# An SSD stage with its sample states turned, C unscaled, and the carried state faded on GpSimd

## The chip, the cores and the metric

The kernel runs on one core of a Trainium2 chip. The metric is the device time of one execution in microseconds (us).

## The reference, cut to what matters

One layer of a decoder trunk is computed for a prompt of 1024 tokens and for 8 samples of one token each: a half-step FFN, a mixer, a second half-step FFN. The mixer has a sparse attention branch and an SSD (state space) branch. The change lies in the SSD branch alone, which is, for 32 heads of 64 in 4 groups, with a state of 128 per head and chunks of 128 tokens:

```python
def step(h, inp):                       # one chunk of 128 tokens
    xc, dtc, Bc, Cc = inp
    acs = jnp.cumsum(dtc * Ar, axis=1)
    seg = acs[:, :, None] - acs[:, None, :]
    decay = jnp.exp(jnp.where(tril, seg, -jnp.inf))
    xdt = xc * dtc[..., None]
    cb = jnp.einsum('blgn,bsgn->blsg', Cc, Bc)
    y_diag = jnp.einsum('blsg,blsgr,bsgrp->blgrp', cb, decay, xdt)
    y_off = jnp.einsum('blgn,bgrpn,blgr->blgrp', Cc, h, jnp.exp(acs))
    to_end = jnp.exp(acs[:, -1:] - acs)
    h_new = jnp.exp(acs[:, -1])[..., None, None] * h + jnp.einsum('bsgn,bsgr,bsgrp->bgrpn', Bc, to_end, xdt)
    return h_new, y_diag + y_off
...
y = y + d_skip[:, None] * xs
y = y.reshape(b, T, D_INNER) * silu(z)
y = group_rmsnorm(y) * norm_ssd
```

A sample is one token on a given state: its state is faded by exp(dt A), B times x dt is added, and the sum with C is its output. The new states are outputs of the kernel.

## The kernel before, in words

The program is a row of phases (FFN, projections and scores, time steps, the dense projections, the SSD stage, gathers, attention, FFN). Between two phases all engines meet at a barrier. Inside a phase each engine has its own program, written out by hand, and engines wait for each other by semaphores with counts; an engine works through its program strictly in order, so the order of the lines is the order of the work. `eng.wait_ge(sem, UP + n)` holds an engine's queue until n events have been counted.

`time_steps` (line 1594) computes dt, the running sums `acs` of dt A inside a chunk, `etot` (the exponential of a chunk's whole sum) and `te`, and stores `acs` turned, by head and token, in DRAM for later.

`ssd_groups` (line 2110) goes through 32 steps, n = 0 to 31: group n // 8, chunk n % 8 (`N = SG * TB`). In a step:

- SP loads the chunk's x, B and C (`st`), the sums `acs` spread over all partitions (`ab`) and the gate (`zt`), and loads and stores sample states (`H`).
- TensorE's `turn` (2242) transposes x and B and forms C times B into pB. `through` (2252) multiplies B with the weighted x into pH, what the chunk adds to the carried state, and then forms the output pY: for each head `xdt` times `E` (inside the chunk) and the carried state `hT` times `Cs` (what came before it). `total` (2271) sums squares for the norm.
- ScalarE's `decays` (2337) makes `E`, the exponentials of the differences, in eight shifts and one exponential, and `Cs`, the exponentials of the sums themselves; `decay` fades a sample state unit in four instructions.
- GpSimd's `weigh` makes `xw`; `scale` (2386) multiplies `Cs` by C for eight heads; `read` (2392) multiplies a sample unit with C.
- VectorE's `enter` (2412) makes `xdt` and cuts C times B to the triangle (`cbm`); `states` (2423) adds pH to the faded state `hd` (its sum is `hT`); `weigh` (2443) multiplies E with cbm; `skip` (2448) adds d_skip times x to pY; `fade` (2434) fades the carried state; `gate`, `update` (2456) and `reduce` (2466) follow.

The sample states are cut into 32 units of 128 partitions (two heads' inner index) by 4 samples by 128 state entries, one unit a step, two steps late (`LAG = 2`). At the end of each group VectorE makes a diagonal of the inverse roots, TensorE spreads it over the partitions (`broadcast`), and VectorE normalises the group. VectorE's order is this:

```python
for i in range(N + LAG + 1):
    enter(i + 2); states(i); weigh(i + 1); skip(i); fade(i + 1)
    gate(i); update(i - LAG); reduce(i - LAG - 1)
    ...
```

(written here without the tests on i that cut the ends off, and `...` for the norms.)

Of the kernel before, what the change touches and what calls it, by code (L numbers as in the profile page):

```python
# [1593 lines left out]
def time_steps(nc, d, o, scr, tok, dt, te, etot, acs, upper, ident, constants):  # L1594
# [3 lines left out]
    with Phase(nc, "ts") as ph:  # L1598
# [4 lines left out]
        turn = ph.sb("turn", [P, 2, P])  # L1603
# [13 lines left out]
        @block.sync  # L1617
        def _(sp):
            sp.dma_start(rows[:, 0], d["dt_bias"]).then_inc(r_in, 16)
            sp.dma_start(rows[:, 1], d["a_log"]).then_inc(r_in, 16)  # L1620
            sp.dma_start(upper[:], d["upper"]).then_inc(r_in, 16)
            for dst, src in constants:
                sp.dma_start(dst[:], d[src]).then_inc(others, 16)
            sp.dma_start(o["conv_old"], d["conv_old"]).then_inc(others, 16)
            sp.wait_ge(moved, UP + 1)
            sp.dma_start(scr["acs"].rearrange("(j q) l -> q j l", j=2), turn[:]).then_inc(stored, 16)
            sp.wait_ge(moved, UP + 2)
            sp.dma_start(scr["steps"].rearrange("v h b -> h v b"), steps[:]).then_inc(stored, 16)
            sp.wait_ge(stored, UP + 32)
            sp.wait_ge(others, UP + 16 * (len(constants) + 1))  # L1630

        @block.scalar
        def _(act):
# [11 lines left out]
            act.wait_ge(exped, UP + 5)  # L1645
# [464 lines left out]
def ssd_groups(nc, d, o, scr, h, S, dt, te, etot, acs, upper, dskip, nssd, smc, zsm, ones, ident):  # L2110
# [4 lines left out]
    N, UNITS = SG * TB, SG * GT * 2  # L2115
    RS, RZ, RH, HB = 4, 3, 4, NB // 2
    LAG = 2
    with Phase(nc, "sg") as ph:
        st = ph.sb("st", [P, RS, XT, P])
        zt = ph.sb("zt", [P, RZ, GT, P])  # L2120
        ab, E, Cs = (ph.sb(n, [P, 2, R, P]) for n in ("ab", "E", "Cs"))
        xdt, xw = (ph.sb(n, [P, 3, GW]) for n in ("xdt", "xw"))
        bt, cbm = ph.sb("bt", [P, 3, 2 * P]), ph.sb("cbm", [P, 2, P])
        hT, hd = (ph.sb(n, [P, 2, GW]) for n in ("hT", "hd"))
        sq = ph.sb("sq", [P, 2, GT, P])
        root, diag = ph.sb("root", [P, N + SG]), ph.sb("diag", [P, TB, P])
        eps = ph.sb("eps", [P, 1])
        H, T = ph.sb("H", [P, RH, HB, DS]), ph.sb("T", [P, 2, HB, DS])
        bc = ph.sb("bc", [P, 2, 2, HB, DS])
        bcs = ph.sb("bcs", [NB, 2, SG, DS])  # L2130
        steps = ph.sb("steps", [P, 2, SG * GT, NB])
        xd, sk, ys, sqs = (ph.sb(n, [P, SG, GT, NB]) for n in ("xd", "sk", "ys", "sqs"))
        diag8 = ph.sb("diag8", [NB, SG, NB])
        pX, pB, pH, pR = (ph.ps(n, [P, 512]) for n in ("pX", "pB", "pH", "pR"))
        pY, pD = ph.ps("pY", [P, 2, 512]), ph.ps("pD", [P, 2, 512])
        st_in = [ph.sem(f"st_in{q}") for q in range(RS)]
        z_in = [ph.sem(f"z_in{q}") for q in range(RZ)]
        ab_in, bc_in = ([ph.sem(f"{n}{q}") for q in range(2)] for n in ("ab_in", "bc_in"))
        H_in, H_out = ([ph.sem(f"{n}{q}") for q in range(RH)] for n in ("H_in", "H_out"))
        yd = [ph.sem(f"yd{x}") for x in range(2)]  # L2140
        turned, x_dt, cb_m, copied, grown, exped, weighed, x_w, c_s, h_d, h_mm, hup, skipped, gated, squared, summed = (
            ph.sem(n) for n in ("turned", "x_dt", "cb_m", "copied", "grown", "exped", "weighed", "x_w", "c_s", "h_d", "h_mm", "hup",
                                "skipped", "gated", "squared", "summed"))
        rooted, inv, diagd, spread, scaled, decayed, updated, multd, reduced, small, rows_t, rows_m, rows_s, ssm_saved, ch_s, tail, fallen = (
            ph.sem(n) for n in ("rooted", "inv", "diagd", "spread", "scaled", "decayed", "updated", "multd", "reduced", "small", "rows_t",
                                "rows_m", "rows_s", "ssm_saved", "ch", "tail", "fallen"))
        block = ph.block()
        flat = lambda a: a.rearrange("p r l -> p (r l)")
        v3 = lambda a: a.rearrange("p (r e) -> p r e", r=R)
        wide = lambda a, n: a[:, n % TB, n // TB * R:(n // TB + 1) * R].unsqueeze(2).to_broadcast([P, R, PD])  # L2150
# [13 lines left out]
        def _(sp):  # L2164
            def chunk(n):
                if n >= RS:
                    sp.wait_ge(skipped, UP + n - RS + 1)
                    sp.wait_ge(c_s, UP + later(n - RS))
                sp.dma_start(st[:, n % RS], scr["xc"][n // TB, n % TB]).then_inc(st_in[n % RS], 16)
# [6 lines left out]
            def sums(n):  # L2176
                if n >= 2:
                    sp.wait_ge(exped, UP + n - 1)
                    sp.wait_ge(grown, UP + later(n - 2))
# [3 lines left out]
            def state(m, io):  # L2183
                g, half, t = unit(m)
                return io[g].rearrange("p (t b e) -> p t b e", t=GT, b=NB)[:, t, half * HB:(half + 1) * HB]

            def load_state(m):
                if m >= RH:
                    sp.wait_ge(H_out[m % RH], UP + 16 * (m // RH))
                    sp.wait_ge(multd, UP + m - RH + 1)  # L2190
                sp.dma_start(H[:, m % RH], state(m, d["state_ssm"])).then_inc(H_in[m % RH], 16)

            def load_rows(k):
                if k >= 2:
# [8 lines left out]
            for v in range(2):  # L2203
                for x in range(2):
                    src = bass.AP(scr["steps"].tensor, (v * SH + x) * NB, [[0, PD], [2 * NB, SG * GT], [1, NB]])
                    sp.dma_start(steps[x * PD:(x + 1) * PD, v], src).then_inc(small, 16)
            for n in range(2, RS):
                chunk(n)
            for n in range(RZ):
# [3 lines left out]
            sp.wait_ge(rows_m, UP + 1)  # L2213
            sp.dma_start(scr["bcs"].rearrange("v g b e -> b v g e"), bcs[:]).then_inc(rows_s, 16)
            sp.wait_ge(rows_s, UP + 16)
            load_rows(0)
            load_rows(1)
            for i in range(N + LAG + 2):
                if 2 <= i + 2 < N:
                    sums(i + 2)  # L2220
                if RS <= i + RS - 1 < N:
                    chunk(i + RS - 1)
                if RZ <= i + RZ - 1 < N:
                    gate(i + RZ - 1)
                m = i - 1 - LAG
                if 0 <= m < UNITS:
                    sp.wait_ge(updated, UP + m + 1)
                    sp.dma_start(state(m, o["ssm_s"]), H[:, m % RH]).then_inc(H_out[m % RH], 16)
                    if m >= 1 and m - 1 + RH < UNITS:
                        load_state(m - 1 + RH)  # L2230
                    if m % GT == GT - 1 and m // GT + 2 < UNITS // GT:
                        load_rows(m // GT + 2)
# [3 lines left out]
            for q in range(RH):  # L2236
                sp.wait_ge(H_out[q], UP + 16 * (UNITS // RH))
# [3 lines left out]
        def _(pe):  # L2241
# [10 lines left out]
            def through(n):  # L2252
                pe.wait_ge(copied, UP + n + 1)
                pe.wait_ge(x_w, UP + n + 1)
                pe.wait_ge(hup, UP + n)
                nc.tensor.matmul(pH[:], bt[:, n % 3, 0:P], xw[:, n % 3], start=True, stop=True).then_inc(h_mm, 1)
                pe.wait_ge(weighed, UP + n + 1)
                pe.wait_ge(c_s, UP + later(n))
                pe.wait_ge(skipped, UP + n - 1) if n >= 2 else pe.wait_ge(rows_m, UP + 1)
                first = n % TB == 0  # L2260
                for t in range(GT):
                    for k in range(1 if first else 2):
                        for x in range(2):
                            r = 2 * t + x
                            lhs, rhs = (xdt[:, n % 3], E[:, n % 2, r]) if k == 0 else (hT[:, (n - 1) % 2], Cs[:, n % 2, r])
                            m = nc.tensor.matmul(pY[PD * x:PD * (x + 1), n % 2, t * P:(t + 1) * P], lhs[:, r * PD:(r + 1) * PD], rhs,
                                                 start=k == 0, stop=first or k == 1)
                            if t == GT - 1 and (first or k == 1):
                                m.then_inc(yd[x], 1)

            def total(n):
                pe.wait_ge(squared, UP + n + 1)
                if n % TB == 0:
                    pe.wait_ge(rooted, UP + n // TB)
# [4 lines left out]
            def broadcast(g):  # L2279
                pe.wait_ge(diagd, UP + TB * (g + 1))  # L2280
                pe.wait_ge(scaled, UP + GT * g)
                for c in range(TB):
                    m = nc.tensor.matmul(pD[:, c // 4, c % 4 * P:(c % 4 + 1) * P], ones[:], diag[:, c], start=True, stop=True)
                m.then_inc(spread, 1)

            for v in range(2):
                for g in range(SG):
                    m = nc.tensor.transpose(pY[0:NB, v, g * P:(g + 1) * P], smc[:, g * XT + GT + v], ident[:])
            m.then_inc(rows_t, 1)
            turn(0)  # L2290
            turn(1)
            for i in range(N + 2):
# [4 lines left out]
                if i >= 2:  # L2297
                    total(i - 2)
                if i >= TB + 5 and (i - 5) % TB == 0 and i <= N:
                    broadcast((i - 5) // TB - 1)  # L2300
# [6 lines left out]
            broadcast(SG - 1)  # L2307
# [5 lines left out]
        def _(act):  # L2313
            def copy(n):
                act.wait_ge(turned, UP + n + 1)
                if n >= 3:
                    act.wait_ge(h_mm, UP + n - 2)
                    act.wait_ge(cb_m, UP + n - 2)
# [7 lines left out]

            def decay(m):
                g, half, t = unit(m)
                act.wait_ge(H_in[m % RH], UP + 16 * (m // RH + 1))
                if m == 0:  # L2330
                    act.wait_ge(small, UP + 64)
                for b in range(HB):
                    at = half * HB + b
# [786 lines left out]
```

## Time and profile before

| | us |
|---|---|
| three runs | 4072.28, 4075.02, 4075.45 (median 4075.02) |
| the profiled execution: its own time | 4073.7 |
| its span, first to last instruction | 4071.9 |
| TensorE busy | 3724.5 (91%) |
| VectorE busy | 1986.9 (49%) |
| ScalarE busy | 943.4 (23%) |
| GpSimd busy | 358.0 (9%) |

The profile page gives one execution. Shares are of the whole span, which has stages with different limits; the SSD stage begins at 2017.9 us, VectorE's last instruction in it starts at 2324.0.
### The profile page before, as it was taken

To read this page: it belongs to the slowest core of one execution; us is meant where nothing else is said; L and a number is where in the kernel's file an instruction comes from. 1 tells how busy PE (TensorE), PEld (TensorE's weight loads), DVE (VectorE), ACT (ScalarE), POOL (GpSimd) and SP (SyncE) were. 2 spreads that over 40 slices of the span, in tenths; PEclk is the share of its full clock that TensorE was granted. 3 is DMA by queue.
4 is the path that set the end of the run, shared out by engine and by line. 5 is a ranking of instruction groups with operands and counts; after the bars stand their busy time and mean duration, and the time that the engine had idled before them with its cause. 6 is when DMAs were issued, how large, how long until landed. Compare 5 with 4: busy or idle time off the path is not lost. (4 is left out here: it accounts for less than half of the span.)

```text
span 4071.9 us, 48044 instructions
## 1 busy us (share of the span) xinstructions
PE 3724.5 (91%) x18116; PEld 2942.2 (72%) x18116; DVE 1986.9 (49%) x4404; ACT 943.4 (23%) x2079; POOL 358.0 (9%) x372
## 2 busy tenths in 40 slices
PE   5999999998996999999777589789899999999997
PEld 3888888885654888888655456445467888888886
DVE  3444444442123888764299732244441354453544
ACT  2111111112131222221377400156300221111111
POOL 0000000000000000000055411354100000000000
PEclk8999999998998999999888699899989999999999
DMA  4333343215441132222367332200114022222222
GB/s 182 121 124 124 117 153 124 103 66 192 115 110 68 53 104 84 83 84 83 101 221 221 114 108 81 71 16 11 60 49 152 11 93 83 83 94 77 90 83 83
DMA packets 178142, 406.45 MB, mean 100 GB/s; under 512 B 25896, under 2 KB 104952, under 8 KB 156648
## 3 DMA queue, kind: packets, MB, share of 16 engines
q1 hardware_dynamic: 162264, 360.48, 26.6%
q10 hardware_dynamic: 12448, 21.78, 1.5%
q0 software_dynamic: 3200, 21.11, 1.4%
q8 instruction: 145, 2.38, 0.2%
q14 instruction: 85, 0.70, 0.1%
HBM read 335.35 MB, written 68.14 MB: 99 GB/s over the span
## 5 line engine op out<-in xcount | busy, mean ns | idle before, releaser
L659 ACT ACTIVATE f_u<-f_Y 128x258 f32<-128x258 f32 x408 | 157.2, 385 | 1093.1 <-PE f_Y L558 1093.1
L785 DVE TENSOR_TENSOR f_g<-f_u,f_Z 128x258 f32<-128x258 f32 x136 | 57.6, 424 | 390.7 <-PE f_Z L558 390.7
L1114 PE MATMUL ps_pp<-h,ps_w 128*128 128x344 f32 x720 | 219.0, 461 | 19.9 <-DMA ps_w<-in_w_att 19.9
L1114 PEld LDWEIGHTS ps_pp<-h,ps_w 128*128 128x128 f32 x720 | 136.0, 192 | 100.2 <-DMA ps_w<-in_w_att 20.3
L755 DVE TENSOR_TENSOR f_g<-f_u,f_X 128x258 f32<-128x258 f32 x136 | 57.6, 423 | 299.3 <-PE f_X L558 293.4
L558 PE MATMUL f_Y<-h,raw 128*128 128x258 f32 x704 | 171.2, 387 | 13.6 <-PEq L111 13.6
L558 PE MATMUL f_Y<-f_a,raw 128*128 128x258 f32 x704 | 170.9, 384 | 6.2 <-issue 6.2
L558 PE MATMUL f_Y<-f_tc,f_sums 128*128 128x258 f32 x704 | 167.5, 380 | 1.9 <-issue 1.2
L558 PE MATMUL f_Y<-f_a,f_sums 128*128 128x258 f32 x704 | 168.8, 380 | 0.0
L558 PE MATMUL f_Y<-f_tc,raw 128*128 128x258 f32 x704 | 167.7, 380 | 0.9 <-ACT f_u L659 0.9
L558 PE MATMUL f_X<-h,raw 128*128 128x258 f32 x704 | 168.1, 382 | 0.0
L558 PE MATMUL f_Y<-h,f_sums 128*128 128x258 f32 x704 | 167.5, 381 | 0.5 <-ACT f_u L659 0.5
L558 PE MATMUL f_Z<-h,f_sums 128*128 128x258 f32 x704 | 167.5, 380 | 0.0
L558 PE MATMUL f_Z<-f_tc,f_sums 128*128 128x258 f32 x704 | 167.5, 380 | 0.0
L558 PE MATMUL f_Z<-f_a,f_sums 128*128 128x258 f32 x704 | 162.9, 380 | 0.0
L558 PEld LDWEIGHTS f_Y<-h,raw 128*128 128x128 f32 x704 | 133.2, 192 | 40.7 <-issue 22.1
L1917 ACT ACTIVATE S<-dn_Y 128x258 f32<-128x258 f32 x168 | 64.4, 383 | 411.6 <-PE dn_Y L1857 411.6
L558 PEld LDWEIGHTS f_Y<-f_a,raw 128*128 128x128 f32 x704 | 133.2, 190 | 29.5 <-issue 10.3
L558 PEld LDWEIGHTS f_Y<-f_tc,f_sums 128*128 128x128 f32 x704 | 132.8, 189 | 22.7 <-issue 2.7
L558 PEld LDWEIGHTS f_Y<-f_tc,raw 128*128 128x128 f32 x704 | 133.1, 189 | 21.5 <-ACT f_u L659 1.8
L558 PEld LDWEIGHTS f_X<-h,raw 128*128 128x128 f32 x704 | 134.3, 191 | 19.6
L558 PEld LDWEIGHTS f_Y<-h,f_sums 128*128 128x128 f32 x704 | 133.2, 189 | 20.7 <-ACT f_u L659 0.9
(433 smaller groups left out, 7356.5 us busy)
## 6 DMA issues: line engine op xcount, KB each, us to landing
raw<-in_w_f1i SPq DMA_DIRECT2D x44, 1024.0 KB, 4.9
raw<-in_w_f2i SPq DMA_DIRECT2D x44, 1024.0 KB, 4.8
f_wa<-in_w_ada SPq DMA_DIRECT2D x14, 2048.0 KB, 9.7
dn_raw<-in_w_dense SPq DMA_DIRECT2D x28, 1024.0 KB, 5.6
raw<-in_w_f1o SPq DMA_DIRECT2D x16, 1024.0 KB, 4.9
sg_ab<-scr_acs SPq DMA_DIRECT2D x32, 512.0 KB, 5.4
raw<-in_w_f2o SPq DMA_DIRECT2D x16, 1024.0 KB, 4.8
scr_xc<-dn_cv SPq DMA_DIRECT2D x24, 512.0 KB, 4.4
```

The lines of the kernel that those rows point to most:

```text
L558: m = nc.tensor.matmul(bank[i % 2][:, 0:SUB], left[:, k], column(i, which, k), start=fresh and k == 0, stop=k == kp - 1, skip_group_check= ...
L659: nc.scalar.activation(u[:, i % 2, n], bank[i % 2][:, 0:SUB], ACT.Copy).then_inc(done, 1)
L755: nc.vector.tensor_tensor(g[:, i % 2, 0], u[:, i % 2, 0], X[i % 2][:, 0:SUB], ALU.add).then_inc(xread, 1)
L785: nc.vector.tensor_tensor(g[:, i % 2, 1], u[:, i % 2, 1], Z[i % 2][:, 0:SUB], ALU.add).then_inc(zread, 1)
L1114: m = nc.tensor.matmul(pp[n % 2][:, 0:NC], w[:, t % WR, k], h[:, k, c * NC:(c + 1) * NC], start=k == 0, stop=k == KT - 1)
L1917: nc.scalar.activation(u[:, i % 2, n], Y[i % 2][:, 0:SUB], ACT.Copy).then_inc(done, 1)
```

## The change

In `time_steps` the turned sums also go through an exponential on ScalarE, and the result is stored beside them (`eacs`). In `ssd_groups`:

- C is no longer scaled: `Cs`, its exponential on ScalarE and its multiply on GpSimd are gone. The carried state times C goes into a bank of its own, pC, four products for the eight heads; VectorE multiplies pC by the stored exponentials (`carried`, loaded by SP's `growth` as `ea`) and adds pY (`join`).
- The skip moves to TensorE: pY begins with a diagonal of d_skip (`dskips`, made on GpSimd once a group) times x. pY has one buffer instead of two.
- The triangle is cut on GpSimd (`cut`), in bt itself.
- The fading of the carried state goes from VectorE to GpSimd.
- A unit of sample states is now one sample of one group, with the state entries on partitions and the 512 inner entries along them. GpSimd fades it in one multiply (`decay`); TensorE forms B times x dt into pU (`grow`, 8 rows deep, with all but one sample's B masked to zero), VectorE adds pU (`update`), and TensorE forms the output, state times C, as columns of pR (`read`). The arrays in DRAM are laid out to match.
- The norm's broadcast goes in two halves through one bank, and ScalarE copies each to SBUF (`keep`). `zt` has two buffers instead of three.

The core of the diff:

```diff
@@ time_steps
+            sp.wait_ge(exped, UP + 6)
+            sp.dma_start(scr["eacs"].rearrange("(j q) l -> q j l", j=2), grown[:]).then_inc(stored, 16)
...
+            act.wait_ge(moved, UP + 1)
+            nc.scalar.activation(grown[:], turn[:], ACT.Exp).then_inc(exped, 1)
@@ ssd_groups, SP
+            def growth(n):
+                k = later(n) - 1
+                if k >= 2:
+                    sp.wait_ge(mulled, UP + k - 1)
+                for x in range(2):
...
+                    sp.dma_start(ea[x * PD:(x + 1) * PD, k % 2], src).then_inc(ea_in[k % 2], 16)
@@ TensorE
+                if n % TB:
+                    pe.wait_ge(mulled, UP + later(n) - 1)
+                    for t in range(GT):
+                        m = nc.tensor.matmul(pC[:, t * P:(t + 1) * P], hT[:, (n - 1) % 2, t * P:(t + 1) * P], st[:, q, GT + 1], start=True, stop=True)
+                    m.then_inc(c_mm, 1)
+                pe.wait_ge(joined, UP + n)
...
+            def grow(m):
+                pe.wait_ge(updated, UP + m)
+                pe.wait_ge(b_masked, UP + m // NB + 1)
+                nc.tensor.matmul(pU[:], bmask[:, m // NB % 2, m % NB], xrow[:, m // NB], start=True, stop=True).then_inc(u_mm, 1)
+            def read(m):
+                pe.wait_ge(updated, UP + m + 1)
+                for t in range(GT):
...
+            for i in range(N + LAG + 2):
                 if i + 2 < N:
                     turn(i + 2)
                 if i < N:
                     through(i)
...
+                if 0 <= i - LAG - 1 < N:
+                    read(i - LAG - 1)
+                if 0 <= i - LAG + 1 < N:
+                    grow(i - LAG + 1)
+                if 2 <= i < N + 2:
                     total(i - 2)
@@ GpSimd
+            for i in range(N + LAG):
                 if i + 2 < N:
+                    cut(i + 2)
                     weigh(i + 2)
                 if i + 1 < N and (i + 1) % TB:
-                    scale(i + 1)
-                if 0 <= i - LAG < UNITS:
-                    read(i - LAG)
+                    fade(i + 1)
+                if i % TB == 3 and i // TB + 1 < SG:
+                    mask_rows(i // TB + 1)
+                if i % TB == 4 and i // TB + 1 < SG:
+                    skip_rows(i // TB + 1)
+                if 0 <= i - LAG + 1 < N:
+                    decay(i - LAG + 1)
@@ VectorE
             def states(n):
                 dve.wait_ge(h_mm, UP + n + 1)
                 dve.wait_ge(h_d, UP + later(n))
-                wait_y(dve, n)
+                dve.wait_ge(c_mm, UP + later(n))
...
+            def update(m):
+                dve.wait_ge(decayed, UP + m + 1)
+                dve.wait_ge(u_mm, UP + m + 1)
+                nc.vector.tensor_tensor(H[:, m % RH], H[:, m % RH], pU[:], ALU.add).then_inc(updated, 1)
...
                 if i < N:
-                    skip(i)
-                if i + 1 < N and (i + 1) % TB:
-                    fade(i + 1)
+                    if i % TB:
+                        carried(i)
+                    join(i)
                 if i < N:
                     gate(i)
-                if 0 <= i - LAG < UNITS:
+                if 0 <= i - LAG < N:
                     update(i - LAG)
```

How the order of instructions changes on two engines. First TensorE, in the loop of `ssd_groups`, from the end of one step's pY to the next step's: before, pR is the sum of squares (`total`), pX and pB the turn, pH the chunk's state (the numbers of stages are semaphores).

```order
L2276 MATMUL sg_pR<-ones,sg_sq 128x1 [waits stage35]
L2276 MATMUL sg_pR<-ones,sg_sq 128x1 x3
L2248 MATMUL sg_pX<-ident,sg_st 128x128 [waits stage24,stage22,stage3]
L2248 MATMUL sg_pX<-ident,sg_st 128x128 x3
L2249 MATMUL sg_pB<-ident,sg_st 128x128
L2250 MATMUL sg_pB<-sg_st 128x128
L2256 MATMUL sg_pH<-sg_xw,sg_bt 128x512 [waits stage32,stage28,stage24]
```

The same place after the change; pR with smc and H is `read`, pU is `grow`, which waits for stage44 (`updated`) and stage50 (`b_masked`), and pC is the carried state times C.

```order
L2283 MATMUL sg_pR<-smc,sg_H 128x1 [waits stage44]
L2283 MATMUL sg_pR<-smc,sg_H 128x1 x3
L2277 MATMUL sg_pU<-sg_xrow,sg_bmask 128x512 [waits stage50,stage44]
L2290 MATMUL sg_pR<-ones,sg_sq 128x1 [waits stage34]
L2290 MATMUL sg_pR<-ones,sg_sq 128x1 x3
L2244 MATMUL sg_pX<-ident,sg_st 128x128 [waits stage23,stage21,stage3]
L2244 MATMUL sg_pX<-ident,sg_st 128x128 x3
L2245 MATMUL sg_pB<-ident,sg_st 128x128
L2246 MATMUL sg_pB<-sg_st 128x128
L2253 MATMUL sg_pH<-sg_xw,sg_bt 128x512 [waits stage29,stage26,stage23]
L2257 MATMUL sg_pC<-sg_st,sg_hT 128x128 [waits stage31]
```

Between pY and the turn, `read` and `grow` have come in ahead of `total`, each behind a wait for VectorE's updates, and pC stands behind pH.

Then VectorE, one step of its loop, before the change, from xdt (`enter`) to the reduction (ys).

```order
L2417 TENSOR_TENSOR sg_xdt<-sg_pX,dt 128x512 [waits stage20,stage28,stage19,stage21]
L2421 TENSOR_TENSOR sg_cbm<-sg_bt,upper 128x128 [waits stage24,stage27]
L2432 TENSOR_TENSOR sg_hT<-sg_hd,sg_pH 128x512 [waits stage19,stage20,stage30,stage31]
L2446 TENSOR_TENSOR sg_E<-sg_E,sg_cbm 128x1024 [waits stage23,stage26]
L2452 SCALAR_TENSOR_TENSOR h<-sg_st,dskip,sg_pY 128x128 [waits stage20,stage19]
L2452 SCALAR_TENSOR_TENSOR h<-sg_st,dskip,sg_pY 128x128 x3
L2436 TENSOR_TENSOR sg_hd<-sg_hT,etot 128x512 [waits stage32]
L2441 TENSOR_TENSOR h<-h,sg_zt 128x4x128 [waits stage4,stage33]
L2462 SCALAR_TENSOR_TENSOR sg_H<-sg_bc,sg_xd,sg_H 128x128 [waits stage10,stage42]
L2462 SCALAR_TENSOR_TENSOR sg_H<-sg_bc,sg_xd,sg_H 128x128 x3
L2469 TENSOR_REDUCE sg_ys<-sg_T 128x4 [waits stage44]
```

After the change: stage30 is `c_mm`, stage31 `mulled`, stage32 `joined`, stages 18 and 19 the two halves of pY.

```order
L2463 TENSOR_TENSOR sg_xdt<-sg_pX,dt 128x512 [waits stage19,stage26,stage18,stage20]
L2474 TENSOR_TENSOR sg_hT<-sg_hd,sg_pH 128x512 [waits stage30,stage27,stage28]
L2479 TENSOR_TENSOR sg_E<-sg_E,sg_bt 128x1024 [waits stage22,stage24]
L2486 TENSOR_TENSOR h<-sg_pC,sg_ea 128x4x128 [waits stage9,stage30]
L2492 TENSOR_TENSOR h<-h,sg_pY 128x4x128 [waits stage31,stage19,stage18]
L2499 TENSOR_TENSOR h<-h,sg_zt 128x4x128 [waits stage4,stage32]
L2504 TENSOR_TENSOR sg_H<-sg_H,sg_pU 128x512 [waits stage43,stage42]
```

The mask, the skip, the fading and the reduction are gone; the state sum waits for pC's end (stage30), and the one add of pU stands last in the step.

## Rows read from the trace of the kernel before

**Rows 1.** Stretches of the SSD stage: us, busy us (instructions) per engine, PEclk, DMA share, GB/s
```profile
2080.00:2120.00 40.00, 29.81 (x261) 22.73 (x261) 39.97 (x80) 34.09 (x85) 24.95 (x15) 0.87 0.75 245
2120.00:2160.00 40.00, 29.49 (x237) 23.36 (x236) 39.97 (x80) 31.88 (x79) 28.05 (x15) 0.87 0.75 211
2160.00:2200.00 40.00, 30.89 (x227) 24.19 (x224) 39.97 (x76) 33.38 (x81) 22.80 (x14) 0.73 0.75 243
2200.00:2240.00 40.00, 28.80 (x241) 21.94 (x241) 39.93 (x83) 30.20 (x78) 22.53 (x14) 0.88 0.72 220
```

**Rows 2.** Timeline of VectorE, one step: start, us, engine, line, operation, out<-in, shapes
```profile
2129.57 0.68 DVE L2432 TENSOR_TENSOR sg_hT<-sg_hd,sg_pH 128x512 f32<-128x512 f32 x1
...
2136.56 0.68 DVE L2417 TENSOR_TENSOR sg_xdt<-sg_pX,dt 128x512 f32<-128x512 f32 x1
2137.16 0.38 DVE L2421 TENSOR_TENSOR sg_cbm<-sg_bt,upper 128x128 f32<-128x128 f32 x1
2137.46 0.68 DVE L2432 TENSOR_TENSOR sg_hT<-sg_hd,sg_pH 128x512 f32<-128x512 f32 x1
2138.06 1.46 DVE L2446 TENSOR_TENSOR sg_E<-sg_E,sg_cbm 128x1024 f32<-128x1024 f32 x1
2139.44 1.11 DVE L2452 SCALAR_TENSOR_TENSOR h<-sg_st,dskip,sg_pY 128x128 f32<-128x128 f32 x4
2140.48 1.81 DVE L2436 TENSOR_TENSOR sg_hd<-sg_hT,etot 128x512 f32<-128x512 f32 x1
2142.21 0.68 DVE L2441 TENSOR_TENSOR h<-h,sg_zt 128x512 f32<-128x512 f32 x1
2142.81 1.13 DVE L2462 SCALAR_TENSOR_TENSOR sg_H<-sg_bc,sg_xd,sg_H 128x128 f32<-128x128 f32 x4
2143.86 0.67 DVE L2469 TENSOR_REDUCE sg_ys<-sg_T 128x4 f32<-128x512 f32 x1
```

**Rows 3.** Timeline of VectorE: the first and the last state sum of the stage
```profile
2038.24 0.69 DVE L2430 COPY sg_hT<-sg_pH 128x512 f32<-128x512 f32 x1
...
2298.72 0.68 DVE L2432 TENSOR_TENSOR sg_hT<-sg_hd,sg_pH 128x512 f32<-128x512 f32 x1
```

**Rows 4.** Timeline of TensorE in the same step
```profile
2137.34 0.63 PE L2248 MATMUL sg_pX<-ident,sg_st 128*128 128x128 f32 x4 [0.45 <-issue]
2137.81 0.27 PE L2249 MATMUL sg_pB<-ident,sg_st 128*128 128x128 f32 x1
2137.92 0.39 PE L2250 MATMUL sg_pB<-sg_st 128*128 128x128 f32 x2
...
2141.84 0.44 PE L2266 MATMUL sg_pY<-sg_E,sg_xdt 128*64 128x128 f32 x4 [2.46 <-issue]
...
2143.74 1.05 PE L2276 MATMUL sg_pR<-ones,sg_sq 128*128 128x1 f32 x8
```

**Rows 5.** Tile E: ns min/median/max of the weighing, first and last start
```profile
L2446 DVE TENSOR_TENSOR sg_E<-sg_E,sg_cbm x32: 1211/1464/2087, 2034.8 to 2291.3; 128x1024 f32<-128x1024 f32 x32
```

**Rows 6.** Timeline of TensorE: the first product of the carried state
```profile
2036.29 1.91 PE L2256 MATMUL sg_pH<-sg_xw,sg_bt 128*128 128x512 f32 x2
```

**Rows 7.** Timeline of GpSimd, the step before
```profile
2129.45 1.09 POOL L2384 TENSOR_TENSOR sg_xw<-sg_xdt,te 128x512 f32<-128x512 f32 x1
2130.51 3.34 POOL L2389 TENSOR_TENSOR sg_Cs<-sg_Cs,sg_st 128x1024 f32<-128x1024 f32 x1
```

**Rows 8.** Timeline of VectorE beside it
```profile
2130.16 1.46 DVE L2446 TENSOR_TENSOR sg_E<-sg_E,sg_cbm 128x1024 f32<-128x1024 f32 x1
...
2132.58 1.81 DVE L2436 TENSOR_TENSOR sg_hd<-sg_hT,etot 128x512 f32<-128x512 f32 x1
```

**Rows 9.** Tile hd: ns min/median/max of the fading
```profile
L2436 DVE TENSOR_TENSOR sg_hd<-sg_hT,etot x28: 680/1805/1816, 2041.3 to 2293.6; 128x512 f32<-128x512 f32 x28
```

**Rows 10.** Line 1097, a triangular cut on GpSimd in another stage: ns min/median/max
```profile
L1097 POOL TENSOR_SCALAR_AFFINE_SELECT mask<-mask x2: 287/288/289, 1036.4 to 1036.6; 128x128 f32<-128x128 f32 x2
```

**Rows 11.** Timeline of TensorE behind the last step
```profile
2298.53 5.28 PE L2276 MATMUL sg_pR<-ones,sg_sq 128*128 128x1 f32 x24
```

More of the change, by code:

```diff
@@ L2127, in ssd_groups @@
+        rb = ph.sb("rb", [P, TB, P])
         eps = ph.sb("eps", [P, 1])
[L2128 to L2132, printed above, removed]
+        H = ph.sb("H", [P, RH, GW])
+        dskips = ph.sb("dskips", [P, 2, GT, P])
+        dab = ph.sb("dab", [P, SH, NB])
@@ L2147, in ssd_groups @@
+        rooted, inv, diagd, spread, kept, scaled, decayed, u_mm, updated, y_mm, small, rows_t, rows_m, skips, b_masked, ssm_saved, ch_s, tail, fallen = (
+            ph.sem(n) for n in ("rooted", "inv", "diagd", "spread", "kept", "scaled", "decayed", "u_mm", "updated", "y_mm", "small", "rows_t",
+                                "rows_m", "skips", "b_masked", "ssm_saved", "ch", "tail", "fallen"))
         block = ph.block()
@@ L2257, in through @@
+                pe.wait_ge(joined, UP + n)
+                if n % TB == 0:
+                    pe.wait_ge(skips, UP + n // TB + 1)
                 pe.wait_ge(weighed, UP + n + 1)
-                pe.wait_ge(c_s, UP + later(n))
-                pe.wait_ge(skipped, UP + n - 1) if n >= 2 else pe.wait_ge(rows_m, UP + 1)
-                first = n % TB == 0
                 for t in range(GT):
[L2262 to L2269, printed above, removed]
+                    for x in range(2):
+                        nc.tensor.matmul(pY[PD * x:PD * (x + 1), t * P:(t + 1) * P], dskips[:, n // TB % 2, t, PD * x:PD * (x + 1)], st[:, q, t],
+                                         start=True, stop=False)
+                    for x in range(2):
+                        r = 2 * t + x
+                        m = nc.tensor.matmul(pY[PD * x:PD * (x + 1), t * P:(t + 1) * P], xdt[:, n % 3, r * PD:(r + 1) * PD], E[:, n % 2, r],
+                                             start=False, stop=True)
+                        if t == GT - 1:
+                            m.then_inc(yd[x], 1)
@@ L2306, in _ @@
             m.then_inc(summed, 1)
-            broadcast(SG - 1)
+            for half in range(2):
+                broadcast(SG - 1, half)
             pe.wait_ge(tail, UP + 3)
@@ new lines, in join, with gate @@
+            def join(n):
+                wait_y(dve, n + 1)
+                if n % TB:
+                    dve.wait_ge(mulled, UP + later(n))
+                    nc.vector.tensor_tensor(y(n), y(n), tiles(pY[:]), ALU.add).then_inc(joined, 1)
+                else:
+                    nc.vector.tensor_copy(y(n), tiles(pY[:])).then_inc(joined, 1)
+            def gate(n):
+                dve.wait_ge(joined, UP + n + 1)
+                dve.wait_ge(z_in[n % RZ], UP + 16 * (n // RZ + 1))
+                nc.vector.tensor_tensor(y(n), y(n), zt[:, n % RZ], ALU.mult).then_inc(gated, 1)
```

283 lines of the change are left out of this document (136 added, 147 removed).

## Prediction

> **What bounds the kernel now.** The chip sees one long chain of stages, most of them TensorE streams. The change touches one of them, the SSD stage, and a few instructions of the time-step stage ahead of it, so I read the SSD stage alone. First the busy time by stretches: VectorE is busy 39.93 to 40.00 of every 40 us, while TensorE, ScalarE and GpSimd each have idle time, and TensorE's granted clock is 0.73 to 0.88 [rows 1]. So VectorE sets the pace. Then VectorE's timeline over one step (one chunk of 128 tokens of one group): the state sum starts at 2129.57 and again at 2137.46, 7.89 us apart, and the nine groups between follow each other without a gap [rows 2]. The first state sum of the stage starts at 2038.24, the last at 2298.72 [rows 3]: 260.5 us for 31 periods, 8.40 each, the extra being the norms at the ends of groups. TensorE's own stream for a step is short at full clock [rows 4], and it waits freely: 2.5 us ahead of the first pY product, for the weights E and the scaled C.
>
> **What the change removes from VectorE.** By the starts in [rows 2]: the masking of CB 0.30, the skip 1.03 (four instructions), the fading 1.73, four update instructions 1.05 and the reduction 0.60, together 4.71. It adds three operations of 512 elements with one operand in PSUM: `carried`, `join` and `update`. The nearest row is the xdt product, also 512 from PSUM, 0.60 from start to start; so 1.8 come back. VectorE's own work per step falls from 7.89 to 4.98. Were VectorE still the bound, 2.9 us a step would be gained. It is not, because of an order that the change writes for TensorE and VectorE.
>
> **The loop that replaces it.** `grow(i-1)` on TensorE waits for `updated` up to i-1, which is `update(i-2)`, as pU is one bank. VectorE does `update(i-2)` last in its step i, behind `states(i)`, `weigh(i+1)`, `carried(i)`, `join(i)`, `gate(i)`; and `states(i)` waits for `c_mm`, the products pC of the same step. Behind `grow(i-1)` on TensorE's queue stand `total(i-2)`, `turn(i+3)`, pH(i+1) and pC(i+1), on which `states(i+1)` waits. So each step goes once through a half on VectorE and a half on TensorE, one after the other. `pY(i)` and `read(i-3)` run beside VectorE's half, and `enter(i+3)` with the norms of a group's end beside TensorE's half.
>
> VectorE's half: states 0.60; weigh 1.21 alone [rows 5], of which its successor overlaps 0.08 (2138.06 plus 1.46 against 2139.44 [rows 2]), so 1.13; `carried` 0.68 and `join` 0.68, since each writes what the next reads and no overlap is left; gate 0.60; update 0.68. Hand-overs between engines or through a semaphore: pH ended at 2038.20 [rows 6] and the state copy began at 2038.24 [rows 3], 0.04; four of them 0.16. Sum 4.53.
>
> One thing lengthens it. `fade(i+1)` on GpSimd is released by `states(i)`, just after weigh has started, and `decay(i-1)` stands behind it. What two SBUF readers do to each other shows in [rows 7, 8]: GpSimd's multiply of 1024 elements began at 2130.51, ended at 2133.85; VectorE's fading began at 2132.58 and ended at 2134.39, 0.54 after GpSimd's end, in 1.81 instead of the 0.68 that it takes alone [rows 9]. An xdt product with one operand in PSUM costs 0.68 beside GpSimd [rows 2]. So from the end of weigh, W, fade runs to W + 1.06 and decay to W + 2.12 (a GpSimd multiply of 512 is 1.06 by the starts in [rows 7]); the gate, two SBUF operands, is ready at W + 1.36, waits 0.76 and then takes 0.54 instead of 0.68: plus 0.62. Half with it: 5.15.
>
> The Trainium skill, page "SBUF — State Buffer", section "SBUF: two separate sides", says that VectorE and GpSimd share one port pair as an exclusive lock, held for a whole instruction, the other blocking fully. The trace agrees (0.54 behind GpSimd's end). By the other reading of 1.81 against 0.68, plain slowing while both run, the gate would take 1.13 more instead of 0.62, and the sum below would be 14 us longer.
>
> TensorE's half at full clock: one pass of 128 columns is 0.11 (pB at 2137.81 and 2137.92 [rows 4]), and the float32 products have two passes each. grow is 512 columns twice, 0.88; total 1.05; turn 7 passes, 0.80; pH 0.88; pC 8 passes, 0.88; the drain of the last pass 0.17 (0.39 less two times 0.11). Sum 4.66. grow has 8 rows and pC another weight each time; I take neither for dearer, as the rows go by columns. At the stage's median clock, 0.87 [rows 1], all but the drain is 4.49 / 0.87 = 5.16: 5.33. I take this one, since pauses remain on TensorE each step.
>
> Period 5.15 + 5.33 = 10.48. The first chunk of groups 1 to 3 lacks pC (1.01) and `carried` (0.72): 8.75. Six half broadcasts stand in TensorE's half, 8 passes each, 1.01. Three `mask_rows` (1024 elements on GpSimd, 2.23 once weigh let go at 2131.62 [rows 7, 8]) go before a decay and hold the gate 1.2 longer each. So 28 x 10.48 + 3 x 8.75 + 6 x 1.01 + 3 x 1.2 = 329.4 against 260.5: **plus 69**.
>
> **What costs nothing, and its cover.** `cut` is 0.29 on GpSimd [rows 10], and xw, fade and decay 3.2; behind a period of 10.5 they have slack, and if the cover went, pH would wait for xw. ScalarE loses C's exponential and the decays. SP gets two more transfers a step (the exponentials, 256 KB) and waits for `carried(i)` ahead of gates and states, but each lands a period before its use; were it late, `carried` would stall next. zt has two buffers instead of three: issued after `carried(i)`, used a period later. The ends of the stage: behind the last state sum stand two more reads, 16 passes at the 0.22 that 24 passes took there (5.28 [rows 11]), 3.5 us; ScalarE's first copy no longer waits for an exponential, and one more store stands in the time-step stage. I take plus 4 in all, between minus 3 (the earlier start alone) and plus 10 (the norm of the last group in halves, one behind the other). Sum 4073.7 + 73 = **4147**. The profiled execution, 4073.7, is 1.3 below the median, 4075.0; the difference is inside what can be told apart, about 0.2% or 8 us.
>
> **Rivals.** (a) *TensorE's stream is the bound, and the wait of grow never ends last*: 0.80 + 0.88 + 0.88 + 1.90 (pY, 2141.84 to 2143.74 [rows 4]) + 1.05 (read, 8 passes as total) + 0.88 + 1.05 = 7.44 at full clock; 28 x 7.44 + 3 x 6.56 + 5.3 = 233, minus 27, with the ends 4050: faster. For it speaks that VectorE has only 4.98 to do. It needs VectorE's half to end while pY and read run, 2.95 against 4.53, so I give it 0.08. (b) *The loop alone*: full clock, no blocked gate: 4.53 + 4.66 = 9.19; 28 x 9.19 + 3 x 7.59 + 5.3 = 285, plus 25, 4099. For it speaks that TensorE is busier per step than before; against it the 0.73 to 0.88 of [rows 1]. 0.17. With the blocked gate at full clock it is 9.81, 4124, inside my case. (c) *TensorE's half at 1.2 GHz in every step*, since each is preceded by a pause: 9.15 + 5.15 = 14.3, plus 190, 4270. No 40 us stretch of [rows 1] is below 0.73; 0.06. (d) VectorE stays the bound or something hides all: the loop would have to be near 8.2; nothing in the program gives that, 0.03. That leaves 0.66 for the forecast.
>
> **How the numbers follow.** Within the forecast, a mean clock of 0.70, below any stretch of [rows 1], gives a period of 11.7, 4190, and with it the upper end of the ends 4200. The low end takes in (b) with something off the ends: 4095. Outside are (a), (c), (d), 0.17, and a little of (b). Faster by over 0.2% is (a), 0.08; within 0.2% is (d), 0.03; slower is the rest, 0.89.
>
> **What would show it.** In the profile after: VectorE no longer full in the SSD stage but idle some 4 us a step ahead of `states`, released by pC; TensorE idle 1.5 to 3 us ahead of the pU product, released by `update`; state sums about 10.5 us apart; the gate 1.2 to 1.4 us long beside GpSimd's decay. If TensorE runs through pU without waiting, if state sums are under 8.2 us apart, or if the gate stays at 0.68, the loop or the lock is wrong.

## The result, and the profile after

The changed kernel takes 4195.51 us (median of 4 runs, 4187.04 to 4199.2); the kernel before, beside it on the same chip, 4075.23 (4072.28 to 4075.95). The ratio is 1.0294, 95% interval 1.0276 to 1.0311: slower, by 120 us where 73 were forecast. The time lies inside the range (4095 to 4200), near its upper end. The profiled execution took 4194.81, its span is 4193.1.

The same four stretches of the SSD stage (columns as in [rows 1]):

```profile
2080.00:2120.00 40.00, 33.83 (x218) 26.50 (x217) 15.91 (x21) 13.22 (x33) 10.97 (x11) 0.76 0.60 193
2120.00:2160.00 40.00, 33.85 (x225) 25.84 (x226) 18.02 (x23) 16.95 (x38) 14.65 (x15) 0.77 0.44 147
2160.00:2200.00 40.00, 33.03 (x229) 26.25 (x226) 19.03 (x27) 13.82 (x35) 16.90 (x15) 0.79 0.58 178
2200.00:2240.00 40.00, 31.51 (x207) 23.95 (x206) 20.61 (x30) 16.09 (x43) 14.54 (x13) 0.79 0.39 122
```

VectorE, full before, is busy for 16 to 21 of 40 us, and TensorE is not full either. Nobody is the bound: engines wait for each other. The tile view of hT gives the state sums (ns min/median/max, first and last start), those of a group's first chunk on a line of their own:

```profile
L2474 DVE TENSOR_TENSOR sg_hT<-sg_hd,sg_pH x28: 678/687/690, 2041.9 to 2413.2; 128x512 f32<-128x512 f32 x28
L2472 DVE COPY sg_hT<-sg_pH x4: 692/692/692, 2036.4 to 2326.5; 128x512 f32<-128x512 f32 x4
```

From 2036.4 to 2413.2 are 376.8 us where [rows 3] had 260.5: plus 116, nearly all of the 120. The mean period is 12.15 us instead of 8.40. VectorE's timeline over one step, columns as in [rows 2], with the idle time ahead and who ended it in brackets:

```profile
2183.88 0.69 DVE L2474 TENSOR_TENSOR sg_hT<-sg_hd,sg_pH 128x512 f32<-128x512 f32 x1 [2.27 <-PE sg_pC L2257]
2184.49 1.22 DVE L2479 TENSOR_TENSOR sg_E<-sg_E,sg_bt 128x1024 f32<-128x1024 f32 x1
2185.62 0.68 DVE L2486 TENSOR_TENSOR h<-sg_pC,sg_ea 128x512 f32<-128x512 f32 x1
2186.44 0.69 DVE L2492 TENSOR_TENSOR h<-h,sg_pY 128x512 f32<-128x512 f32 x1
2187.16 1.01 DVE L2499 TENSOR_TENSOR h<-h,sg_zt 128x512 f32<-128x512 f32 x1
2188.09 0.67 DVE L2504 TENSOR_TENSOR sg_H<-sg_H,sg_pU 128x512 f32<-128x512 f32 x1
2195.19 0.69 DVE L2463 TENSOR_TENSOR sg_xdt<-sg_pX,dt 128x512 f32<-128x512 f32 x1 [6.42 <-PE sg_pB L2246]
2197.86 0.69 DVE L2474 TENSOR_TENSOR sg_hT<-sg_hd,sg_pH 128x512 f32<-128x512 f32 x1 [1.98 <-PE sg_pC L2257]
```

And TensorE's timeline in the same step:

```profile
2185.57 1.05 PE L2283 MATMUL sg_pR<-smc,sg_H 128*128 128x1 f32 x8
2188.82 1.12 PE L2277 MATMUL sg_pU<-sg_xrow,sg_bmask 8*128 8x512 f32 x2 [2.19 <-DVE sg_H L2504]
2189.87 1.87 PE L2290 MATMUL sg_pR<-ones,sg_sq 128*128 128x1 f32 x8
2191.60 2.05 PE L2297 MATMUL sg_pD<-sg_diag,ones 128*128 128x128 f32 x8
2193.45 1.06 PE L2244 MATMUL sg_pX<-ident,sg_st 128*128 128x128 f32 x4
2194.30 0.42 PE L2245 MATMUL sg_pB<-ident,sg_st 128*128 128x128 f32 x1
2194.51 0.64 PE L2246 MATMUL sg_pB<-sg_st 128*128 128x128 f32 x2
2194.94 1.89 PE L2253 MATMUL sg_pH<-sg_xw,sg_bt 128*128 128x512 f32 x2
2196.65 1.07 PE L2257 MATMUL sg_pC<-sg_st,sg_hT 128*128 128x128 f32 x8
```

The loop of the prediction stands there: the last pC ends, VectorE runs from states to update, pU waits 2.19 us for that update, then total, broadcast, turn, pH and pC pass, and only then come the next states. VectorE's half is 4.94 us (2183.88 to 2188.82; forecast 5.15). TensorE's half is 9.04 (to 2197.86), of which 1.85 are a half broadcast. But look at the durations. `total` takes 1.87 here; `read`, eight passes of the same shape ahead of the pause, took 1.05, as `total` did in [rows 4]. Four passes of pX take 1.06 instead of 0.63. The groups of TensorE between 2080 and 2400 us (count, busy us, mean ns of one, idle before) say the same for all steps:

```profile
L2253 PE MATMUL sg_pH<-sg_xw,sg_bt 128*128 128x512 f32 x52 | 48.7, 1040 | 0.0
L2290 PE MATMUL sg_pR<-ones,sg_sq 128*128 128x1 f32 x208 | 40.4, 316 | 0.0
L2269 PE MATMUL sg_pY<-sg_E,sg_xdt 128*64 128x128 f32 x404 | 39.5, 274 | 0.0
L2277 PE MATMUL sg_pU<-sg_xrow,sg_bmask 8*128 8x512 f32 x52 | 32.0, 698 | 56.7 <-DVE sg_H L2504 56.7
L2283 PE MATMUL sg_pR<-smc,sg_H 128*128 128x1 f32 x200 | 26.3, 253 | 0.0
L2244 PE MATMUL sg_pX<-ident,sg_st 128*128 128x128 f32 x100 | 25.9, 411 | 0.0
```

pY and read, which run ahead of the pause beside VectorE's half, are at full speed. What runs behind the pause, in TensorE's half, is at half speed for much of it. Here are VectorE's and TensorE's half of the step above, then of a step without a broadcast, as stretches (the granted clock is the third number from the end):

```profile
2183.88:2188.82 4.94, 2.75 (x40) 2.49 (x37) 4.71 (x6) 0.00 (x0) 2.97 (x2) 1.00 0.17 52
2188.82:2197.86 9.04, 9.04 (x39) 7.13 (x41) 0.70 (x2) 4.14 (x11) 0.00 (x0) 0.62 0.95 268
2235.39:2240.33 4.94, 2.67 (x41) 2.42 (x37) 4.77 (x7) 3.06 (x9) 2.97 (x2) 1.00 0.14 42
2240.33:2248.41 8.08, 8.08 (x31) 5.89 (x33) 1.83 (x2) 2.89 (x5) 1.34 (x2) 0.58 0.71 221
```

So the stage's mean granted clock of 0.77 is no even 0.77: the 1.2 GHz level falls on the half that sets the period. Over all plain steps (no broadcast, no group's first chunk; 24 of them) the median from the start of pU to the next state sum is 7.84 us and the mean 7.39, at a granted clock of 0.64 in the mean; in VectorE's halves of the same steps it is 0.99. Nearly all of these TensorE halves come in two lengths, some 6.5 us at a clock of 0.74 and some 8 us at 0.57 to 0.60.

Two waits carry the loop in the view of waits from 2080 to 2400 (us, times, longest):

```profile
DVE sg_hT L2474 <- PE sg_pC L2257: 60.3, 23, 6.7
...
PE sg_pU L2277 <- DVE sg_H L2504: 56.7, 26, 3.0
```

GpSimd's timeline beside VectorE's half, and the gate of the first two groups (ns min/median/max):

```profile
2184.65 1.96 POOL L2419 TENSOR_TENSOR sg_hd<-sg_hT,etot 128x512 f32<-128x512 f32 x1 [1.91 <-DVE sg_hT L2474]
2186.57 1.05 POOL L2414 TENSOR_TENSOR sg_H<-sg_H,sg_dab 128x512 f32<-128x512 f32 x1
```

```profile
L2499 DVE TENSOR_TENSOR h<-h,sg_zt x16: 691/1007/1848, 2040.7 to 2214.9; 128x512 f32<-128x512 f32 x16
```

Weigh ends at 2185.71. The fading, released during it, ends 0.90 later; the decay ends at 2187.62; the gate, ready at 2187.16, ends 0.55 behind the decay. That is the blocked gate as it was worked out, with the lock of the Trainium skill's page "SBUF — State Buffer", section "SBUF: two separate sides". Three overlaps of different length speak for a lock and against plain slowing. The fading on VectorE in [rows 7, 8] stood 1.27 us beside GpSimd, the fading here 1.06 beside weigh, the gate 0.46 beside the decay; each ended 0.13 to 0.14 sooner behind the blocker than it takes alone (0.54 against 0.68, 0.90 against 1.03, 0.55 against 0.69), however long the overlap was.

### The profile page after: what moved, and what is told of

The parts are those of the page before. It is cut to its first block and busy times, and to the rows that moved or that the text cites. A ratio compares the mean times of both kernels' runs of the same rounds, so it can differ in the third digit from the quotient of the medians.

```text
span 4193.1 us, 48865 instructions
## 1 busy us (share of the span) xinstructions
PE 3860.8 (92%) x18736; PEld 3047.9 (73%) x18736; DVE 1917.9 (46%) x4151; ACT 886.5 (21%) x1932; POOL 340.4 (8%) x412
```

## The experiments

Theory: the loop through `update` and `grow` sets the period, and TensorE's half of it runs mostly at 1.2 GHz. Rivals: something else that the change brought is slow (the blocked gate, the fading on GpSimd, TensorE's own stream), or the low clock is a companion that costs little. Ratios below are to the kernel before, timed beside each (medians 4073.17 to 4075.52).

**The loop cut: update ahead of states.** VectorE does `update(i - 2)` before it waits for pC.

```diff
                     enter(i + 2)
+                if 0 <= i - LAG < N:
+                    update(i - LAG)
                 if i < N:
                     states(i)
...
-                if 0 <= i - LAG < N:
-                    update(i - LAG)
```

> The update of the sample state is put ahead of the state sum in VectorE's step, where VectorE waits for pC anyway. Loop theory: TensorE's wait ahead of pU (2.2 us a step in the changed kernel) is gone, its stream of 7.4 us a step at full clock becomes the bound, nearly without pauses, so the clock rises too: state sums 7.4 to 8.2 us apart instead of 12.2, total 4045 to 4075. Rival, the products of this stage run at a mean clock near 0.77 whatever stands around them: 7.4 / 0.77 = 9.7 a step, total near 4120. Rival, the wait at pU only shows what another wait would show: state sums stay above 11, total above 4160.

Measured: 4070.35 us (10 runs), ratio to before 0.9994 [0.9984, 1.0003]. The whole loss is gone by one line moved. Three stretches of it:

```profile
2080.00:2120.00 40.00, 40.00 (x315) 30.76 (x312) 25.60 (x33) 22.97 (x56) 18.20 (x17) 0.87 0.65 221
2120.00:2160.00 40.00, 39.22 (x319) 30.96 (x317) 28.47 (x42) 19.43 (x48) 23.81 (x21) 0.87 0.82 267
2160.00:2200.00 40.00, 39.43 (x315) 30.59 (x317) 30.97 (x36) 24.89 (x59) 21.89 (x19) 0.91 0.60 197
```

TensorE is now full, and the wait at pU has left the view of waits. The state sums:

```profile
L2474 DVE TENSOR_TENSOR sg_hT<-sg_hd,sg_pH x28: 673/686/689, 2040.1 to 2292.1; 128x512 f32<-128x512 f32 x28
L2472 DVE COPY sg_hT<-sg_pH x4: 683/688/692, 2035.4 to 2234.1; 128x512 f32<-128x512 f32 x4
```

They lie 8.28 us apart on average. This looks like rival (a) of the prediction, with its 7.44 us of TensorE work at a granted clock of 0.87 to 0.91 instead of 1: the whole gain on VectorE ends in a new bound just where the old one was. Whether TensorE's work alone is that bound is asked again below.

**What stands in TensorE's half: total ahead of grow.** The eight passes of `total(i-2)` go into the pause; nothing else moves.

```diff
-                if 0 <= i - LAG + 1 < N:
-                    grow(i - LAG + 1)
                 if 2 <= i < N + 2:
                     total(i - 2)
+                if 0 <= i - LAG + 1 < N:
+                    grow(i - LAG + 1)
```

> The sums of squares go ahead of the wait at pU on TensorE, from the half of the loop into the pause (2.2 us). If that half runs at 1.2 GHz, its 8 passes are worth 1.87 us a step there: 28 times, 52 us, total near 4143 or lower if the filled pause also raises the clock. If it ran at full clock, 1.05 a step: 29 us, total near 4166. Rival, the wait at pU does not end last: no change, 4195.

Measured: 4142.65 us (ratio 1.0169 [1.0152, 1.0186]), 52.9 below the change: 1.7 us for each of 31 periods. At full clock `total` is 1.05, which would be worth 33 us. In the group view above its 8 passes took 40.4 us in 26 steps, 1.55 each, between the 1.05 of the one level and the 1.87 of the other; 31 of these are 48 us. TensorE's halves of all steps together fell by just that, from 223.6 to 175.4 us, and VectorE's stayed (147.7 and 147.2). The median plain TensorE half fell from 7.84 to 5.60.

**Work that is not needed, in the pause.** Four products of 256 columns into pX (free at that point) are added ahead of `grow`. Their result is overwritten.

```diff
+                if 2 <= i < N - 2:
+                    pe.wait_ge(x_dt, UP + i + 3)
+                    for j in range(4):
+                        nc.tensor.matmul(pX[:, 0:TB * SH], ones[:], te[:].rearrange("p c h -> p (c h)"), start=True, stop=True)
                 if 0 <= i - LAG + 1 < N:
                     grow(i - LAG + 1)
```

> Four extra products of 256 columns (8 passes, 1.8 us at full clock), whose result nothing reads, are put in TensorE's pause between the read and pU. Nothing else changes. Clock theory: the half of the loop on TensorE runs at 1.2 GHz because it follows the pause; with the pause filled it runs at 2.4 GHz, 4.7 to 5.3 us instead of about 7, state sums 10 to 10.6 us apart, total 4130 to 4150, faster with more work. Rival, the products of that half are dearer in themselves (8 rows deep, new weights each time): the half stays near 7 us, total 4190 to 4200, or later by what the extra products overrun the pause.

Measured: 4138.19 us (ratio 1.0167 [1.0147, 1.0186]). With 2 us more work a step on TensorE the kernel is 57.3 us faster than the change. TensorE's timeline over a step with a broadcast, to be held against the one above (the next chunk here is a group's first, so there is no pC):

```profile
2184.11 1.97 PE L2321 MATMUL sg_pX<-te,ones 128*128 128x256 f32 x8
2186.01 1.12 PE L2277 MATMUL sg_pU<-sg_xrow,sg_bmask 8*128 8x512 f32 x2
2187.07 1.05 PE L2290 MATMUL sg_pR<-ones,sg_sq 128*128 128x1 f32 x8
2187.98 1.14 PE L2297 MATMUL sg_pD<-sg_diag,ones 128*128 128x128 f32 x8
2188.95 0.60 PE L2244 MATMUL sg_pX<-ident,sg_st 128*128 128x128 f32 x4
...
2189.72 1.02 PE L2253 MATMUL sg_pH<-sg_xw,sg_bt 128*128 128x512 f32 x2
```

`total` is back from 1.87 to 1.05, the broadcast from 2.05 to 1.14, pH from 1.89 to 1.02. The granted clock in the stretches from 2080 to 2280 is 0.94 to 1.00. The median plain TensorE half is 4.82 us, where the prediction worked out 4.66 for full clock; VectorE's half is 4.94 in the median as before. So the clock theory holds with the sign that no other theory gives.

**The blocked gate.** GpSimd's decay goes between `cut` and xw, away from the gate.

```diff
                     cut(i + 2)
+                if 0 <= i - LAG + 1 < N:
+                    decay(i - LAG + 1)
+                if i + 2 < N:
                     weigh(i + 2)
...
-                if 0 <= i - LAG + 1 < N:
-                    decay(i - LAG + 1)
```

> GpSimd's decay of the sample state goes ahead of its xw, away from VectorE's gate; the fading stays where it is. Lock theory: the gate takes 0.68 instead of 1.01 us, 28 steps shorter by 0.33, total 4183 to 4190. Rival, the gate is slowed by something else than the decay: gate stays near 1.0, total 4193 to 4199.

Measured: 4190.05 us (ratio 1.0282 [1.0264, 1.0299]), 5.5 below the change. The intervals overlap, so the time alone tells little; the gate tells more:

```profile
L2500 DVE TENSOR_TENSOR h<-h,sg_zt x16: 691/692/1845, 2039.3 to 2212.1; 128x512 f32<-128x512 f32 x16
```

Its median went from 1007 to 692 ns, so the cause of the long gate is shown. It is worth little: the expected 0.33 us a step would be 9 us, but some gates stayed long (the longest 1845 ns), and VectorE's halves together fell by 4.0 us.

**The fading back on VectorE**, behind `join`, GpSimd left with cut, xw and decay.

```diff
-                if i + 1 < N and (i + 1) % TB:
-                    fade(i + 1)
...
                     join(i)
+                if i + 1 < N and (i + 1) % TB:
+                    fade(i + 1)
                 if i < N:
                     gate(i)
```

> The fading of the carried state goes back to VectorE, behind the join, all else as changed. Loop theory with the lock: VectorE's half gains the fading, 0.60 to 0.68 us, and loses the blocked gate, 0.33, since GpSimd's decay then runs earlier: plus 0.3 a step, total 4200 to 4212. Rival, the fading on GpSimd is itself what slows the loop: total clearly below 4190.

Measured: 4208.74 us (ratio 1.0327 [1.0311, 1.0343]), 13 above the change (the two intervals just touch). By this the move to GpSimd was a small gain by itself, even though the fading takes 1.96 us there beside weigh: it lies off the loop. Of the loss, VectorE's halves have 7.1 us, close to the expected 0.3 a step; another 8.6 are in TensorE's halves, whose granted clock was lower (0.61 in plain steps against 0.64).

**Can the cut loop be bettered?** Four kernels start from the early update. The first adds the moved decay; the second gives the skip back to VectorE, so that pY has 16 passes instead of 32; the third does both.

```diff
-                    for x in range(2):
-                        nc.tensor.matmul(pY[PD * x:PD * (x + 1), t * P:(t + 1) * P], dskips[:, n // TB % 2, t, PD * x:PD * (x + 1)], st[:, q, t],
-                                         start=True, stop=False)
...
+            def skip(n, other):
+                for t in range(GT):
+                    at = n // TB * GT + t
+                    v = nc.vector.scalar_tensor_tensor(out=y(n)[:, t], in0=st[:, n % RS, t], scalar=dskip[:, at:at + 1],
+                                                       in1=other[:, t], op0=ALU.mult, op1=ALU.add)
+                return v
```

> The early update and the moved decay together. TensorE is the bound with the early update (busy 39 to 40 of 40 us), so a shorter gate on VectorE buys nothing: total 4066 to 4074. Rival, the gate still stands in a loop: 9 us less, near 4061.

> The early update, and d_skip times x back on VectorE (four instructions between carried and join), so that pY has 16 passes instead of 32. TensorE's stream falls from 7.4 to 6.5 us a step at full clock, VectorE's work rises from 5.0 to 6.1. If TensorE stays the bound at the same granted clock (0.87 to 0.91): 1.0 us a step less, total 4037 to 4050, under the kernel before. Rival, TensorE then pauses for VectorE and its clock falls: total 4060 to 4080.

> As the one before with the decay moved ahead of xw on GpSimd as well. If VectorE's work counts again (6.1 us and the norms), the free gate is worth some of its 0.33 us a step: 4030 to 4050, up to 8 below the one before. Rival: no difference between the two.

Measured: 4075.71 (1.0002 [0.9993, 1.0012]), 4088.72 (1.0026 [1.0015, 1.0037]) and 4086.3 (1.0026 [1.0017, 1.0035]). The moved decay gains nothing in the cut loop. Half of pY taken off TensorE made the kernel slower, against an expected gain of 20 to 30 us; the time is above the range of the rival too (4060 to 4080). Two stretches of the second kernel:

```profile
2080.00:2120.00 40.00, 35.87 (x198) 26.49 (x197) 28.07 (x46) 20.23 (x49) 16.18 (x17) 0.73 0.67 217
2120.00:2160.00 40.00, 39.12 (x247) 29.88 (x245) 33.21 (x53) 20.43 (x49) 21.62 (x19) 0.80 0.66 220
```

The clock fell to 0.73 to 0.85. VectorE's step grew too, more than planned: four skips took 2.00 us, beside GpSimd's fading and decay.

```profile
2189.22 2.00 DVE L2477 SCALAR_TENSOR_TENSOR S<-sg_st,dskip,S 128x128 f32<-128x128 f32 x4
```

The fourth kernel tells these two apart: the early update with the 16 skip passes left out (the removed lines above) and nothing in their place.

> The kernel with the early update, with the 16 skip passes of pY left out and nothing in their place: the output lacks d_skip times x, so its time is that of a kernel without this term. It splits the miss of the kernel in which VectorE adds the skip (4088.72 us, granted clock 0.73 to 0.85). Theory 'VectorE': that kernel lost because four skip instructions of 2.0 to 3.6 us made VectorE's step long. Then TensorE, 16 of some 68 passes lighter (at 0.11 us each and the early-update kernel's granted clock of 0.89, 2.0 us of a step), ends its step at 6.3 us and the total falls by 31 x 2.0 to about 4010 (4000 to 4030). Rival 'clock': TensorE with fewer wide passes is granted less clock whoever adds the skip; then the clock in the stage is 0.75 to 0.85 again, with TensorE's work of 5.6 us at full clock taking some 7.5 us with its pauses, and the total stays at 4045 to 4070.

Measured: 4077.82 us (ratio 1.001 [1.0001, 1.0019]). The time is above both ranges, and far above the 4000 to 4030 of the theory that blamed VectorE: even with nobody adding the skip, half of pY is worth nothing. The stretches:

```profile
2080.00:2120.00 40.00, 40.00 (x247) 30.35 (x246) 25.32 (x34) 21.66 (x55) 20.02 (x19) 0.79 0.66 221
2120.00:2160.00 40.00, 34.95 (x219) 26.43 (x218) 26.16 (x39) 21.61 (x52) 20.33 (x19) 0.81 0.77 240
2160.00:2200.00 40.00, 38.10 (x239) 28.65 (x238) 27.73 (x34) 20.94 (x49) 19.26 (x18) 0.81 0.60 202
```

In these the clock is lower than with all passes; in the next two it is 0.91 and 0.89, the mean of the 200 us 0.84 against 0.89. And TensorE waits again: it is busy for 182.25 of the 200 us, 197.90 with all passes; in 17.3 us pX waited for the chunk's load, where the kernel with all passes waited 2.1. So the freed passes went in part to a lower clock and in part to waits. How much each takes, and why the loads come later, stays open. One rival for the floor that these kernels do not get under was not tested, the loads themselves: from 2080 to 2280 us the core's transfers kept its DMA engines 69% busy with all passes and without the 16, and a chunk's load took 6.1 and 6.2 us from issue to landing (medians).

**The one-column passes spread.** In the early-update kernel `read`, with the wait for ScalarE's roots that stands ahead of it, goes between pH and pC, `total` between pC and pY.

```diff
                 nc.tensor.matmul(pH[:], bt[:, n % 3, 0:P], xw[:, n % 3], start=True, stop=True).then_inc(h_mm, 1)
+                first()
...
                     m.then_inc(c_mm, 1)
+                second()
```

> The kernel with the early update, with the four one-column passes of the sample read put between pH and pC and the four of total between pC and pY, so that the eight no longer stand together after pY; all work is the same. Theory 'order': the eight one-column passes and the weight loads between them, standing together, are what holds the granted clock at 0.87 to 0.91 in the early-update kernel. Then the clock rises to 0.95 or more, TensorE's step of 8.28 us shortens by 0.4 to 0.7 us, and the total is 4048 to 4058, below both kernels. Rival 'amount': it is the amount of work that sets the clock, or the passes' order costs waits of its own; then the clock stays and the total is 4065 to 4080.

Measured: 4082.94 us (4072.9 to 4095.84, 12 runs; ratio 1.0026 [1.0015, 1.0037]). The clock rose in only two of five stretches (0.87, 1.00, 0.87, 0.96, 0.87), and TensorE was busy for 36.4 of 40 us instead of 39.6: what the clock gave, new waits took, among them 8.3 us in which `read`, and pC behind it, waited for ScalarE's roots, and 9.5 in which pX waited for loads. (That profiled execution took 4073.89, near the lowest of its runs.) No version that was run beats the kernel before; the early update equals it.

## Why the prediction was right in sign and short in size

- *VectorE is the bound before and will not be after.* Right: full before, about half busy after.
- *The loop update, grow, turn, pH, pC, states sets the period.* Right, and shown: both waits are there, and the loop cut by one moved line takes 125 us off.
- *VectorE's half 5.15.* Measured 4.94 as the median. The lock at the gate is right (0.55 behind the decay's end, 0.54 forecast); the gate was 0.32 longer than alone, not 0.62, since the fading ended 0.90 after weigh instead of 1.06 and the gate was ready 0.09 later. Where `mask_rows` stands ahead of the decay, the half was 5.78, 0.84 more and not 1.2.
- *TensorE's half: 4.66 at full clock, 5.33 at clock 0.87.* This is the step that failed. 4.66 was a good figure for full clock (4.82 in the kernel with the filled pause). But "all but the drain is 4.49 / 0.87" spread the stage's mean clock evenly over TensorE's work, and took that mean from a trace in which TensorE was not on the path. The 1.2 GHz level fell behind the pause, on this half, while pY and read ahead of the pause ran at 2.4 GHz. With the clock of this half itself, 0.64, the same formula gives 7.2. Measured were 7.84 in the median and 7.39 in the mean, between 5.33 and the 9.15 of rival (c), which had the mechanism right and its extent too large.
- *The sum for the stage, 329.4.* 376.8 came, and the 47 us between them are the 47 that the total is off (120 against 73). But 47 is a net. TensorE's halves of the 30 periods with a pU add up to 223.6 us, where the forecast has 163: 61 too few. VectorE's add up to 147.7 against 156, and the first period, which has no pU, took 5.5 against 10.5: together 13 too many. That the time lies inside the range owes something to these terms, which hid a part of the miss.
- *A half broadcast 1.01.* 1.85 in the step shown, for the same reason. Only five of the six counted stand between the first and the last state sum; the last begins at 2421.5.
- *The ends plus 4.* The total moved by 120, the state sums by 116: right as a net. The first state sum came 1.9 us earlier than before; the parts behind the last one were not priced singly. (Rival (b)'s 4099 leaves this plus 4 out, which rival (a)'s 4050 has.)
- *Rival (a), TensorE's stream, 4050.* The kernel with the early update comes near it, at 4070; the clock of 0.89 fits the difference (7.44 / 0.89 = 8.36 against 8.28 measured). That TensorE's work alone is its bound is not shown, since 16 passes less gave nothing.
- *What costs nothing.* The view of waits from 2080 to 2400 us has no wait of TensorE or VectorE for cut, xw, fade or a transfer; the fading on GpSimd was worth 13 us against the run with it on VectorE.

## What to carry to other kernels

Before a gain on the busiest engine is counted, follow the slowest loop of waits of the new order through all engines, and look for one instruction that stands last in one engine's step and first in another's: here moving it (`update` ahead of `states`) took off 125 us, all that the change had cost. Where TensorE's part of such a loop begins behind a pause, price it with rows that ran behind pauses, not with the stage's mean granted clock; and put movable passes into the pause rather than behind it (53 us here).

## What the runs showed of the hardware that was not expected

- Useless work can shorten a kernel: 1.97 us of products a step in TensorE's pause took 57 us off, because `total`, broadcast, turn and pH behind it ran at 2.4 instead of 1.2 GHz (1.87 to 1.05 us for `total`).
- Taking work off a full TensorE can give nothing: with 16 of its passes a step gone, its mean granted clock from 2080 to 2280 us was 0.84 instead of 0.89 and its waits 18 us instead of 2, and the time did not fall (4077.82 against 4070.35).
- GpSimd is blocked by VectorE as well as the other way round: the fading took 1.96 us beside weigh, 1.03 at its shortest, and ended 0.90 after weigh, though it had been released just after weigh began.
